# One prefill-and-decode step of a hybrid layer: queries projected already turned, key gathers in another place, decode states in row groups, one store for the sample

## The reference: what is computed

```
z = (rmsnorm(x) * norm1_g) @ w_in            # columns: rq rk rv rg (retention), mq mk mv (attention)
ret  = retention(rotary(rq), rotary(rk), rv) # 4 heads of 128; prompt from zero, sample from state_ret
attn = block_sparse_softmax(mq, mk, mv, paged cache)   # 8 heads of 64; sample reads 2048 past tokens
mix  = concat(groupnorm(ret) * ret_norm_g * silu(rg), attn)
h = x + mix @ w_out
h = h + top4_of_32_experts(rmsnorm(h) * norm2_g)       # clamped SwiGLU, gate-up 1024x2048, down 1024x1024
y = rmsnorm(h) * final_norm_g
```

## Time and profile before

| | |
|---|---|
| runs of the kernel | 1218.15, 1219.9, 1221.4 us (median 1219.9) |
| the profiled execution | 1218.39 us |
| its span, first to last instruction | 1216.5 us |
| busy: PE / PEld / DVE / ACT / POOL | 1183.0 / 507.0 / 382.6 / 237.2 / 67.9 us |
| bytes moved | 500.64 MB, mean 412 GB/s |
| granted TensorE clock | 0.997 of full |

### The profile page before, as it was taken

One profiled execution on the slowest core, in us unless ns is written; L12 is line 12 of the kernel. 1 busy time (PEld: TensorE's weight loads), 2 busy tenths in 40 slices (PEclk: granted clock), 3 DMA queues, 4 the chain that ended last, 5 costly groups with the idle time before them and its releaser, 6 DMA issues.

```text
span 1216.5 us, 17289 instructions
## 1 busy us (share of the span) xinstructions
PE 1183.0 (97%) x7276; PEld 507.0 (42%) x7276; DVE 382.6 (31%) x541; ACT 237.2 (20%) x561; POOL 67.9 (6%) x70
## 2 busy tenths in 40 slices
PE   8999999999999999999999999999999999999996
PEld 4555545545343443434343434434343434343432
DVE  5999984434112122111111111211111111111113
ACT  3121263423011112112110102111111111110112
POOL 3222112320000000000000000000000000000000
PEclk9999999999999999999999999999999999999998
DMA  9999999999999999999999999999999999999996
GB/s 351 411 378 400 373 360 385 397 400 348 414 430 427 428 428 427 429 429 429 427 429 429 426 431 427 428 429 428 429 427 429 428 427 429 427 428 429 427 423 256
DMA packets 50570, 500.64 MB, mean 412 GB/s; under 512 B 5736, under 2 KB 6400, under 8 KB 19424
## 3 DMA queue, kind: packets, MB, share of 16 engines
q1 hardware_dynamic: 42720, 430.22, 84.6%
q0 software_dynamic: 7520, 69.47, 14.1%
q10 hardware_dynamic: 288, 0.34, 0.1%
HBM read 495.29 MB, written 4.72 MB: 411 GB/s over the span
## 4 chain that ended last, share of the span: by engine, by line
PE 67%; DMA 22%; DVE 5%; issue 3%; ACT 1%; SPq 0%; DVEq 0%
PE psum L1066 24%; DMA arena<-w_gate_up 18%; PE psum L1097 14%; PE psum L959 6%; PE psum L556 3%; DVE arena L1668 3%; DMA arena<-w_down 3%; PE psum L979 3%; PE psum L965 2%; PE psum L648 2%; PE psum L991 2%; PE psum L777 2%; PE psum L998 1%; DMA arena<-w_in 1%; PE psum L475 1%
## 5 line engine op out<-in xcount | busy, mean ns | idle before, releaser
L1066 PE MATMUL psum<-arena 128*64 128x512 f32 x1920 | 421.5, 594 | 11.7 <-DMA arena<-w_gate_up 11.7
L1066 PEld LDWEIGHTS psum<-arena 128*64 128x64 f32 x1920 | 135.0, 137 | 294.6 <-issue 267.8
L2016 DVE TENSOR_SCALAR arena<-psum 128x512 f32<-128x512 f32 x32 | 22.1, 692 | 674.6 <-PE psum L1066 635.6
L1097 PE MATMUL psum<-arena 128*64 128x512 f32 x960 | 212.6, 595 | 0.0
L1246 ACT ACTIVATE arena<-psum 64x512 f32<-64x512 f32 (+6 forms) x193 | 97.6, 509 | 388.1 <-PE psum L1097 170.7
L1668 DVE STREAM_TRANSPOSE arena<-arena 128x2048 f32<-128x2048 f32 x32 | 121.3, 3946 | 0.4 <-DMA arena<-cache_k,arena 0.3
L1097 PEld LDWEIGHTS psum<-arena 128*64 128x64 f32 x960 | 66.2, 136 | 124.3 <-issue 122.5
L556 PE MATMUL psum<-arena 128*128 128x512 f32 x224 | 103.2, 604 | 1.6 <-DMA arena<-w_in 0.9
L1521 ACT ACTIVATE arena<-arena 128x512 f32<-128x512 f32 x30 | 18.9, 631 | 412.3 <-DVE arena L2016 412.3
L959 PE MATMUL psum<-arena 128*128 128x128 f32 x512 | 76.8, 293 | 0.2 <-DVE arena L1928 0.2
L959 PEld LDWEIGHTS psum<-arena 128*128 128x128 f32 x512 | 66.4, 199 | 16.7 <-issue 12.7
(11 more groups left out here) (261 smaller groups left out, 696.5 us busy)
## 6 DMA issues: line engine op xcount, KB each, us to landing
arena<-w_gate_up SPq DMA_DIRECT2D x128, 2048.0 KB, 30.7
arena<-w_down SPq DMA_DIRECT2D x60, 2048.0 KB, 31.6
arena<-w_in SPq DMA_DIRECT2D x6, 2048.0 KB
arena<-w_down SPq DMA_DIRECT2D x7, 1024.0 KB, 35.7
arena<-w_out SPq DMA_DIRECT2D x2, 2048.0 KB
arena<-w_in SPq DMA_DIRECT2D x2, 1024.0 KB, 9.1
out<-arena POOLq DMA_DIRECT2D x1, 2048.0 KB, 19.6
out<-arena SPq DMA_DIRECT2D x3, 512.0 KB, 3.1
```

Of the source, the lines that this page charges most:

```text
L1066: last = mm(psum[64 * g:64 * (g + 1), b, :], xt[:, 2 * kk + m, lhs], gate_slot[slot][:, m, c:c + 512], start=False, stop=kk == 3 and m == ...
L1097: last = mm(psum[64 * g:64 * (g + 1), 2, :], at_sb[:, m, SLOTS * q:SLOTS * (q + 1)], down_slot[slot][:, m, 512 * g:512 * (g + 1)], start=q ...
```

## The change

It has six parts. (a) The prompt's queries come out of the projection turned: `turned_queries` takes the columns of w_in as the stationary side and the 256 tokens as the moving side, so that four banks (two of ring `A`, two of ring `V`) hold mq as `mq_t` needs it, and the eight transposes of the prompt's two tiles fall away. A factor per token can no longer be multiplied when the bank is read (tokens are columns now), so the prompt's scores lack 1/rms, and the softmax takes it as scale and bias of its exponential (`stat[:, 20:24]`). (b) Block 0 runs the first halves of all four column groups, then the sample's queries (bank 7), then the second halves, and key units 0 and 1 are scored inside them. (c) Half of the 16 copies into `qk` go to ScalarE, as 16 smaller ones. (d) POOL may issue key unit 2 when the first half of block 0 has landed, and no longer waits for the second. (e) The sample's states are made two heads at a time: values and keys of head h lie on the partitions 32h to 32h+31, the products of two heads use different row groups of TensorE and write to different banks, and one POOL instruction makes all four `v_blk`. Three copies on VectorE bring the keys there. (f) One transfer stores the sample.

```diff
-            prompt_part(0, 0)
-            q_bank = A.bank()
-            mark["q_sample"] = (a_full, sample_part(0), q_bank)
-            mq = prompt_part(0, 1)
-            mark["block0"] = (a_full, A.n)
+            def turned_queries(c, half):
+                for k in range(4 * half, 4 * half + 4):
+                    last = mm(psum[:, turned_banks[c], 0:LP], win[:, 0, k, c * P:(c + 1) * P], h_t[:, k, 0:LP],
+                              start=k == 0, stop=k == KC - 1)
+                if half == 1:
+                    (A if c < 2 else V).filled(last)
+            pe.wait_ge(block0_half, 16)
+            for c in range(4):
+                turned_queries(c, 0)
+            pe.wait_ge(win_in[0], 16)
...
+            last.then_inc(q_full, 1)
+            for c in range(4):
+                if c == 3:
+                    k_unit(0)
+                    k_unit(1)
+                    units_done[0] = 2
+                turned_queries(c, 1)
+            mark["block0"] = (d_full, V.n)
...
-            slot_transposes(0)
+            slot_transposes(0, (2,))
...
-                    pool.wait_ge(win_in[0], 16)
+                    pool.wait_ge(block0_half, 16)
...
-                                           bias=pm[:, 16 + b:17 + b], scale=SCALE,
+                                           bias=pm[:, 16 + b:17 + b], scale=stat[:, 20:21],
...
+            dve.wait_ge(kdec_ready, 1)
+            for h in range(1, RH):
+                ins = v.tensor_copy(k_dec[NS * h:NS * (h + 1), 2, 0, :], k_dec[0:NS, 2, h, :])
+            ins.then_inc(kgrp_ready, 1)
...
-                    last = mm(psum[:, V.bank(), :], k_dec[0:NS, 2, h, :],
-                              v_blk[0:NS, 4 * half:4 * half + 4, :], start=True, stop=True)
+            def sample_states(two, half):
+                for h in (2 * two, 2 * two + 1):
+                    rows = slice(NS * h, NS * (h + 1))
+                    V.wait_empty(pe)
+                    last = mm(psum[:, V.bank(), :], k_dec[rows, 2, 0, :],
+                              v_blk[rows, 4 * half:4 * half + 4, :], start=True, stop=True)
+                    V.filled(last)
...
-            v_block(0)
-            v_set(12)
-            v_set(13)
-            v_block(1)
-            v_set(14)
-            v_set(15)
-            v_block(2)
-            v_block(3)
+            v_blocks()
+            for n in range(12, 16):
+                v_set(n)
...
-            store_sample(sp, (0, 1))
-            sp.wait_ge(stored, 112)
+            sp.dma_start(outs[1].rearrange("s i (j c) -> j (s i) c", j=4),
+                         y_out[:, 2, 0:256]).then_inc(stored, 16)
+            sp.wait_ge(stored, 64)
```

More of the change, by code:

```diff
@@ L117, in shape_constants @@
     put("own_mask", own.reshape(P, -1))
[L118 removed]
+    put("seq_mask", np.tile((seq[:, None] == np.arange(SEQS)[None]) * 1.0, (RH, 1)))
     valid = np.ones((P, TILES))
@@ L451, in build_kernel @@
         V_SETS = PAGES
-        K_AT = {(0, 1): (5,), (1, 0): (2, 7), (1, 1): (5,), (2, 0): (1, 5), (2, 1): (2, 7), (3, 0): (1, 7),
+        K_AT = {(1, 0): (2, 7), (1, 1): (5,), (2, 0): (1, 5), (2, 1): (2, 7), (3, 0): (1, 7),
                 (3, 1): (4,), (4, 0): (0, 6), (4, 1): (4,), (5, 0): (1, 6)}
[L454 to L460, removed]
+        assert 2 * sum(map(len, K_AT.values())) == K_UNITS - 2
         @block.tensor
@@ L568, in prompt_part, with slot_transposes @@
                 return n
-            def slot_transposes(slot):
+            def slot_transposes(slot, tiles):
                 return [transposes(A, [z[0:COLS[tile], slot, tile, c * P:(c + 1) * P] for c in range(4)],
-                                   COLS[tile]) for tile in range(TILES)]
-            prompt_part(0, 0)
-            q_bank = A.bank()
-            mark["q_sample"] = (a_full, sample_part(0), q_bank)
-            mq = prompt_part(0, 1)
-            mark["block0"] = (a_full, A.n)
+                                   COLS[tile]) for tile in tiles]
+            turned_banks = [ring.banks[(ring.n + i) % 2] for ring in (A, V) for i in range(2)]
+            def turned_queries(c, half):
[8 more added lines that the diff above has]
+            pe.wait_ge(win_in[0], 16)
+            for k in range(KC):
+                for j in range(4):
+                    last = mm(psum[NS * j:NS * (j + 1), 7, 0:P], h_t[:, k, LP:TOK],
+                              win[:, 0, k, j * P:(j + 1) * P], start=k == 0, stop=k == KC - 1)
+            last.then_inc(q_full, 1)
[6 more added lines that the diff above has]
+            mark["block0"] = (d_full, V.n)
+            mark["turned_q"], mark["turned_banks"] = V.n, turned_banks
             prompt_part(1, 0)
@@ L1258, in evacuate_sample, with evacuate_sample_values @@
                 A.emptied(ins)
+            def evacuate_sample_values():
+                A.wait_full(act)
+                copy(z_rv[:, 2, 0:P], psum[:, A.bank(), 0:P])
+                for j in range(1, 4):
+                    ins = copy(z_rv[0:NS, 2, P * j:P * (j + 1)], psum[NS * j:NS * (j + 1), A.bank(), 0:P])
+                A.emptied(ins)
             def evacuate_scaled(dst, w, tile, chunks, gains):
@@ L1343, in evacuate_sequence @@
                 copy(o_raw(seq // 4)[:, seq % 4, :], psum[:, 6 + seq % 2, :]).then_inc(o_evac[seq % 2], 1)
-            evacuate_block(z[:, 0])
             act.wait_ge(qt_ready, 1)
-            evacuate_sample(z[0:NS, 0, 2, :])
-            evacuate_block(z[:, 0], 1)
+            act.wait_ge(qk_zero, 1)
+            for s in range(2, 4):
+                for c in range(4):
+                    for u in range(2):
+                        ins = copy(qk_heads(c)[32 * s:32 * (s + 1), :, u, :, s:16:4], q_heads(c)[:, s, :, u])
+            ins.then_inc(qk_ready, 1)
+            for j in range(4):
+                ins = copy(z[0:NS, 0, 2, P * j:P * (j + 1)], psum[NS * j:NS * (j + 1), 7, 0:P])
+            ins.then_inc(q_copied, 1)
+            for c in range(2):
+                A.wait_full(act)
+                A.emptied(copy(mq_t[:, c, 0:LP], psum[:, A.bank(), 0:LP]))
+            for c in range(2, 4):
+                act.wait_ge(d_full, mark["turned_q"] + c - 3)
+                copy(mq_t[:, c, 0:LP], psum[:, mark["turned_banks"][c], 0:LP]).then_inc(d_empty, 1)
             evacuate_scores(0)
@@ L1398, in _ @@
                 s = s_prompt[:, 8 + 2 * h:10 + 2 * h, :]
-                ins = nc.scalar.activation(s, s, ACT.Exp, bias=pm[:, 24 + h:25 + h], scale=SCALE,
+                ins = nc.scalar.activation(s, s, ACT.Exp, bias=pm[:, 24 + h:25 + h], scale=stat[:, 21:22],
                                            accum_out=pm[:, 40 + h:41 + h])
@@ L1845, in _, with new_states @@
             dve.sem_inc(st2_ready, 1)
-            def new_states(h):
-                for half in range(2):
+            def new_states(two, half):
+                for h in (2 * two, 2 * two + 1):
                     V.wait_full(dve)
@@ L2312, in _ @@
             sp.wait_ge(ret_ready, 1)
-            sp.wait_ge(*mark["vblk3"])
+            sp.wait_ge(*mark["states"])
             load_turn(3)
```

75 lines of the change are left out of this document (35 added, 40 removed).

## The result

The changed kernel takes 1223.28 us (median of 14 runs, 1221.76 to 1225.83) against 1219.93 (14 runs) before: ratio 1.0031, 95% interval 1.0023 to 1.0039. It is slower by 0.3%, beyond the interval; 1213.9 was forecast, with 1211.0 to 1218.5 as the range. The profiled execution has a span (first to last instruction) of 1220.8 us for 1216.5.

The account below looks back on a forecast made before the run. The weights' stream was taken to set the end, moving with TensorE's start of the experts. 2.4 - 0.7 + 3.2 + 1.1 = 6.0 us off the profiled 1218.4 gave 1212.4, on the median's scale 1213.9; range 1211.0 to 1218.5.

Parts of the forecast that it names:

- the first part: What bounds the kernel: the weights' stream sets the end, which moves with TensorE's start of the experts; TensorE has 15.2 us to spare.
- Rival 6: Experts' loop on TensorE: the list's changed length may make it fetch late; 1228.8 us at 2 more a pair; chance 0.06.
- The start of unit 2: Block 0, parts a to d: VectorE starts turning key unit 2 at 27.5 us, 2.4 us sooner.
- the estimated 22.9: Block 0's weights: the second half lands at 22.9 us, if half of 0.84 MB is still to come behind the gathers.
- rival 1: Block 0: the second half block is not late, 3.9 us gained for 2.4, so 1212.4; chance 0.14.
- The copies of the keys: Part e, VectorE at the turned retention keys: three copies and a wait lose 0.7 us (0.5 to 0.9).
- The states: Part e, TensorE's sample states: two heads side by side take 1.0 us; 3.2 us gained in all.
- The store: Part f, the kernel's end: one transfer for the sample gains 1.1 us (0.6 to 1.9).
- rival 4: The sample's store at the end runs on few DMA engines: 0.9 of the 1.1 us gone, 1214.8; chance 0.14.

Follow-up runs that it names:

- e8: The changed kernel with its experts' loop moved as in e1, plus three unused 128x512 products on TensorE at each loop pass's start: 1218.86 us.
- e9: The changed kernel with the experts' loop on TensorE unrolled, fifteen pairs one behind the other and no jump back: 1220.15 us.
- e3: e1 with VectorE's three copies of the retention keys placed behind the reading of the turned keys and heads: 1214.37 us.
- e1: The changed kernel with 210 more instructions, waits met at once, in TensorE's list ahead of the experts' loop: 1216.12 us.
- e4: e3 with the sample stored in four transfers, two from SyncE and two from ScalarE, in place of one: 1213.87 us.
- e2: The kernel before with 46 more instructions, waits met at once, in TensorE's list ahead of the experts' loop: 1226.64 us, 1.0057 of before.

## Why the prediction was wrong

**The step that failed** is in the first part and was carried into the sum: that the end moves with the moment at which TensorE starts the experts. It holds only if the stretch behind that moment keeps its length. In the eight traces without fetches it does: the experts start between 292.70 and 297.54 us, and the stretch is 854.8 to 855.8. But the change lengthened it by 6.2 us. Rival 6 had the place (the list ahead of the loop changes length, a loop that lies badly may fetch late), with a chance of 0.06, and the wrong price. It reckoned with TensorE's time, 15.2 us to spare, and let the case decide from 1.65 us a pair. TensorE lost less than those 24.8: 9.2 us of waits, and 1.7, 3.3 and 3.3 us behind three of the four, where the bias products and the next 64 records took 16.6, 18.3 and 18.3 us for the 15.0 behind the fourth, so 17.5 over fifteen pairs. In a stretch of 861.5 it has 861.5 - 15 x 56.01 = 21.4 to spare; e8 shows that 10.8 are free, and e9 that the fetches cost without any such loss. The engine to price them on was the full one: 16 DMA engines at 1.01. I also took `place_loop` for a pad that counts, and it puts nothing in the list.

**What sets the border** the runs show only from outside: a loop of 1747 instructions was fetched once and kept in two lists up to 21 instructions apart and in a third 255 further on, and fetched anew on each pass in two that lie 45 and 46 on; e8's loop of 1760, 241 on, was kept too.
The Trainium skill has on Runtime: NRT & Kernel Launch (section "Instruction fetch mechanics") that instructions come in 16 KiB blocks of 256, that TensorE holds 2048 of them, and that a jump to a target outside the present window of two blocks must wait for its fetch. The traces agree with the packets' size, and in the changed kernel with the wait (2.1 to 2.5 us); they do not agree with the window, since in the kernel before the same loop jumps back without a fetch (no packet on q8 from 450 to 1150 us).
By estimate from the Trainium skill's 256 a block, 255 more instructions put the loop where it was but for one, and 1747 instructions touch at most eight blocks wherever they begin, which are its 2048: by these figures the loop would be held in either place, and they do not say why nine packets come for each jump back.
No record names a block, so the cause of the border stays open.

**The terms of the sum.** The start of unit 2: 2.5 us sooner for 2.4, and that the two agree so closely is luck. In the three traces of the form before it starts at 29.58 to 31.23, in the seven of the changed form with part d at 26.80 to 29.59, on the mean 2.1 sooner. The 27.37 came by other steps than the 27.5: TensorE began 0.95 later, the queries took 1.95 and not 2.6, and VectorE started 2.66 after them and not 2.0. Whether the half block lands at the estimated 22.9 this trace can't tell, since TensorE came to it at 22.8; in e9 TensorE came at 21.77 and did not wait. So rival 1 (it is not late) is what happened, with its gain used up by the later beginning. The copies of the keys: 2.4 us lost for 0.7. The wait grew by 0.84, near the estimate; the term missed the granted clock, which fell behind the longer wait and cost 1.56 more. e3 showed both. The states: 226.02 to 252.50 before, 226.08 to 249.66 after, so 2.9 gained for 3.2, with the new wait at 0.86 for 0.9. The store: nothing for 1.1, as rival 4 had it and a little worse.
The sum up to the experts is therefore 2.5 - 2.4 + 2.9 = 3.0, of which 2.7 arrived; then 6.2 lost in the experts, and 0.8 in the tail (65.2 us from the last pair to the end, 64.35 before): 4.3 slower, the 1216.5 and 1220.8 of the two spans (the medians are 3.35 apart).

**What was right** shows once the loop lies well: e1, the change as it stands but for the place of the loop, has 1216.1, so 3.4 gained of the 6.0 forecast. With the copies out of the way e3 and e4 have 1214.4 and 1213.9. That this is the 1213.9 of the forecast is luck: e3 has the copies in another place, e4 has no part f, and the term for the store was wrong.

**Open.** Why a fetch costs 0.17 to 0.19 us. By the sum of bytes the weights lost 1.31 MB in 700 us, 3.1 us at 428 GB/s, some 3.8 over the stretch; the rest may be that a part can be used only when its slowest engine has brought its share. The records don't tell one engine's packets from another's, so this is argued and not shown. What speaks for it is what q1 still has to bring from the start of the last pair to the end of the span, before and in the changed kernel:

```profile
q1 hardware_dynamic: 2654, 21.74, 81.0%
```

```profile
q1 hardware_dynamic: 2607, 20.55, 75.6%
```

So 1.19 MB more, 2.8 us at 428 GB/s, had already been brought when the pair could start, and yet its stretch was 6.2 us longer. The eight traces without fetches have 21.6 to 22.0 MB left there, the three with them 20.3 to 20.8. The 0.8 us in the tail were not followed either: e2, with the same fetches, has 64.4 there, and e8, without, 65.1.

## What to carry to other kernels

A loop on an engine whose list was lengthened by a few dozen instructions far ahead of it is to be looked at again: compare the packets on the instruction queue inside the loop before and after, and where there are new ones, move the loop by adding or taking away instructions before judging the change itself. Price everything that moves bytes on the queue that is full, not on the engine that waits. And where a short wait on TensorE grows, look at the granted clock behind it before taking the wait's length as the cost.

## What the runs showed of the hardware that was not expected

- 46 waits that are met at once, placed ahead of a loop, cost 7 us some hundred us later (1226.64 for 1219.52), by 36 fetches of 16 KB of instructions; 210 of them cost nothing that shows (e1).
- A wait of 1.56 us on TensorE was followed by 3.3 us at a mean granted clock of 0.56, one of 0.72 at the same place by none (1.00). Of the four waits of 2.1 to 2.5 at the loop's start, three were followed by some 17 us at a mean of 0.90, 0.81 and 0.81, and one by a clock of 1.00.
- Two products of 32 rows each on different row groups and banks took 1.13 us together (1.05 to the next product) where the same four records took 1.95 on one row group.
- One store of 128 KB and four of 32 KB reach the end of the span alike, 4.6 to 4.7 us behind the first issue.
